# A two-block transformer kernel: one pass of squares for the norms between the blocks, and the context's tiles beside the second mixer's attention steps

## The reference

```python
def rmsnorm(x, g):
    return x * lax.rsqrt(jnp.mean(x * x, -1, keepdims=True) + EPS) * g

# first block, layer i = 1 (layer 0 has a gated short convolution in the place of the stick part)
p = rmsnorm(x, mix_norm[1]) @ b_in                     # 12 heads of stick queries, 4 of memory queries
kv = rmsnorm(x, kv_norm) @ w_kv_shared                 # stick keys and values
z = q @ k.T * scale                                    # stick-breaking attention, causal
log_not = where(causal, log_sigmoid(-z), 0)
tail = reversed_cumsum(log_not) - log_not
y_main = where(causal, exp(log_sigmoid(z) + tail), 0) @ v
y_mem = softmax(q_mem @ mem_k.T * scale) @ mem_v       # memory attention, 4 heads of 64
x = x + concat([y_main, y_mem]) @ w_o[1]
x = x + swiglu(rmsnorm(x, ffn_norm[1]), w_gate[1], w_up[1], w_down[1])
x = rmsnorm(x, final_norm)                             # end of the first block

# second block
sh1x, sc1x, ... = split(silu(c) @ w_ada + b_ada)       # six modulations of x,
sh1c, sc1c, ... = split(silu(c_ctx) @ w_ada + b_ada)   # two that matter of the context
hc = rmsnorm(ctx, norm1_g) * (1 + sc1c) + sh1c
s_f, s_b = context_states(hc)                          # lr, k and v projections of hc, a decayed sum
hx = rmsnorm(x, norm1_g) * (1 + sc1x) + sh1x
x = x + g1x * token_mixer(hx, s_f, s_b)                # begins with lr, k, q, v projections of hx
x = x + g2x * conv_ffn(rmsnorm(x, norm2_g) * (1 + sc2x) + sh2x)
return rmsnorm(x, final_norm_g)
```

## Time and profile before

| what | value |
|---|---|
| median of 3 runs (lowest, highest) | 1211.57 us (1210.45, 1211.79) |
| the profiled execution, its time | 1211.49 us |
| its span in the trace | 1210.2 us |
| PE busy | 1157.9 us, 96% |
| DVE busy | 833.1 us, 69% |
| ACT busy | 622.6 us, 51% |
| POOL busy | 149.4 us, 12% |
| granted TensorE clock, mean | 0.984 |
| DMA | 221.90 MB, mean 183 GB/s |

### The profile page before, as it was taken

One profiled execution on the slowest core, in us unless ns is written; L12 is line 12 of the kernel. 1 busy time (PEld: TensorE's weight loads), 2 busy tenths in 40 slices (PEclk: granted clock), 3 DMA queues, 4 the chain that ended last, 5 costly groups with the idle time before them and its releaser, 6 DMA issues.

```text
span 1210.2 us, 21837 instructions
## 1 busy us (share of the span) xinstructions
PE 1157.9 (96%) x9014; PEld 1110.4 (92%) x9014; DVE 833.1 (69%) x1278; ACT 622.6 (51%) x938; POOL 149.4 (12%) x111
## 2 busy tenths in 40 slices
PE   7999999999899899999999999999999989999996
PEld 6999999999788789999998898979899988999995
DVE  5677677778774756877787756577646767677775
ACT  5655444445564645444455664656437444555553
POOL 0003000000100012000000000000001032344431
PEclk9999999999999989999999999999999997999999
DMA  8655587776744144877877445354324552556550
GB/s 310 195 163 178 165 295 253 240 246 229 244 128 136 51 157 146 263 263 252 274 265 232 160 157 166 105 174 140 114 95 158 185 182 90 186 178 192 175 157 36
DMA packets 60467, 221.90 MB, mean 183 GB/s; under 512 B 6752, under 2 KB 7008, under 8 KB 59984
## 3 DMA queue, kind: packets, MB, share of 16 engines
q1 hardware_dynamic: 59904, 219.06, 55.0%
q10 hardware_dynamic: 288, 1.05, 0.2%
q0 software_dynamic: 176, 0.39, 0.1%
HBM read 219.42 MB, written 1.05 MB: 182 GB/s over the span
## 4 chain that ended last, share of the span: by engine, by line
PE 81%; DVE 10%; ACT 5%; issue 3%; DMA 1%; SPq 0%; POOL 0%; ACTq 0%; DVEq 0%
PE PS L350 23%; PE PS L352 22%; PE PS L351 22%; PE PS L355 13%; DVE w_lo L1316 4%; ACT w_hi L837 3%; DVE PS L1889 1%; DVE SQ L1587 1%; DMA ARENA<-memT 1%; DVE raw L1338 0%; DVE SQ L1352 0%; DVE ARENA L1352 0%; PE PS L455 0%; DVE H_lo L1362 0%; ACT ARENA L925 0%
## 5 line engine op out<-in xcount | busy, mean ns | idle before, releaser
L1316 DVE TENSOR_TENSOR w_lo<-raw,w_hi 128x1024 fp32r<-128x1024 f32 x325 | 398.8, 1228 | 259.9 <-ACT w_hi L837 259.4
L837 ACT ACTIVATE w_hi<-raw 128x1024 fp32r<-128x1024 f32 x356 | 372.5, 1054 | 141.7 <-PE PS L352 117.4
L350 PE MATMUL PS<-Y_hi,w_hi 128*128 128x256 f32 x1240 | 358.4, 289 | 9.6 <-DVE w_lo L1316 4.2
L351 PE MATMUL PS<-Y_lo,w_hi 128*128 128x256 f32 x1240 | 353.9, 285 | 0.0
L352 PE MATMUL PS<-Y_hi,w_lo 128*128 128x256 f32 x1240 | 353.8, 285 | 0.0
L350 PEld LDWEIGHTS PS<-Y_hi,w_hi 128*128 128x128 f32 x1240 | 240.8, 194 | 16.2 <-issue 9.4
L351 PEld LDWEIGHTS PS<-Y_lo,w_hi 128*128 128x128 f32 x1240 | 241.2, 194 | 0.4 <-issue 0.2
L352 PEld LDWEIGHTS PS<-Y_hi,w_lo 128*128 128x128 f32 x1240 | 241.0, 194 | 0.0
L350 PE MATMUL PS<-H_hi,w_hi 128*128 128x256 f32 x808 | 232.1, 287 | 5.3 <-DVE w_lo L1316 2.8
L351 PE MATMUL PS<-H_lo,w_hi 128*128 128x256 f32 x808 | 229.3, 284 | 0.0
L352 PE MATMUL PS<-H_hi,w_lo 128*128 128x256 f32 x808 | 229.2, 284 | 0.0
(11 more groups left out here) (206 smaller groups left out, 1316.7 us busy)
## 6 DMA issues: line engine op xcount, KB each, us to landing
raw<-stream SPq DMA_DIRECT2D x404, 512.0 KB, 4.2
ARENA<-memT SPq DMA_DIRECT2D x2, 512.0 KB, 7.7
X<-xT SPq DMA_DIRECT2D x1, 1024.0 KB, 11.4
ARENA<-c_rows SPq DMA_DIRECT2D x2, 512.0 KB, 8.2
ARENA<-memT SPq DMA_DIRECT2D x1, 1024.0 KB, 7.1
ARENA<-ctxT SPq DMA_DIRECT2D x1, 1024.0 KB, 8.1
outT<-ARENA SPq DMA_DIRECT2D x2, 512.0 KB, 2.6
CROW<-c_rows SPq DMA_DIRECT2D x1, 512.0 KB, 10.2
```

The lines of the kernel that those rows point to most:

```text
L350: pe.matmul(o, wh, xh, start=start, stop=False, skip_group_check=True)
L351: pe.matmul(o, wh, xl, start=False, stop=False, skip_group_check=True)
L837: act.activation(w_hi[n % RING][:], raw[at][:], ACT.Copy).then_inc(*mark("hi", n))
L1316: dve.tensor_tensor(w_lo[n % RING][:], raw[raw_of("slot", n)][:], w_hi[n % RING][:], ALU.subtract).then_inc(*mark("lo_dve", n))
```

## The change

**Tiles.** `ctx_lr` and `ctx_k` (5 slots) move from behind `ffn1` to behind `kv_v1`, where stick groups are still under way. `stick_output` becomes a paced generator `stick_outputs` (banks 2 and 3 instead of 4 to 6) that runs beside `stick_schedule`; `both(...)` steps two generators at once. `w_o1` takes its chunks in the order 0, 1, 2, 3, 6, 7, 4, 5.

**Memory attention** goes in halves: two maxima, two reciprocals, each transposed head waits for its own scalings, and the 8 exponentials are one step of ACT. `memory_attention(1)` starts at the first `b_q` tile, beside the norm of `kv`, and the stick groups now start at the first `kv_k` tile on every engine.

**Context.** The load of the context is issued among the slots of `a_c`; its sum of squares is beside `a_b`; its norm is behind the memory's in the tail of `ffn0`, which begins at j = 16 instead of 18, into memory of its own (`CX_hi`, `CX_lo`). All 16 modulations with two rows are the first 16 of `ffn0`; the second load and second silu of `CTX_ROW` in `ffn1` are gone.

**End of the first block.** `block1_end` takes one pass of squares. The weights of the sum, `PAIR`, are 1 in 16 columns and the square of the final norm's gain in 16 more, so that each quarter holds the sum of x^2 and of (gain x)^2; two matmuls with `HALVES` spread them. From both, ACT and DVE form the two inverse roots, and `norm1` is taken straight from X, with gain times final gain. The final norm of X itself (8 DVE operations) is `block1_output`, beside `context_states`. The norm stands beside 8 tiles (`ctx_v0`, `ctx_v1`) where 13 were.

```diff
-          ("kv_v1", 2), ("w_o1", KC), ("ffn1", FFN_SLOTS),
-          ("ctx_lr", 1), ("ctx_k", 4), ("ctx_v0", 4), ("ctx_v1", 4),
+          ("kv_v1", 2), ("ctx_lr", 1), ("ctx_k", 4), ("w_o1", KC), ("ffn1", FFN_SLOTS),
+          ("ctx_v0", 4), ("ctx_v1", 4),
...
+    if _l == 0:
+        _now = [_j] if _j < CTX_MODS else []
     else:
-        _now = [CTX_MODS + _one + i for i in range(2 if _l and _j in (11, 13, 15, 17) else 1)]
+        _now = [len(MOD_ORDER) + _i for _i in range(2 if _j % 2 and _j > 2 else 1)]
...
+def both(first, second):
+    live = [first, second]
+    while live:
+        live = [task for task in live if next(task, "end") != "end"]
+        if live:
+            yield
...
-                if (kind, n) == ("slot", AT["w_o1"] + RAW):
-                    sp.wait_ge(*past("am", NG - 1))
-                    sp.dma_start(CTX_ROW, c_rows[:, 1]).then_inc(*mark("c_in", 2, by=16))
-                if (kind, n) == ("slot", AT["b_qm"] + RAW - 1):
+                if (kind, n) == ("slot", AT["a_c"] + 4):
                     sp.dma_start(CTX, ctxT).then_inc(*mark("ctx_in", by=16))
...
             def memory_attention(l):        # PE
-                yield from nothing(6)
-                pe.wait_ge(*past("ma_prob", l, 7))
-                claim(*bs)
                 for h in range(MEMH):
+                    if h % 2 == 0:
+                        yield from pace.to(7 + l + h // 2)
+                    pe.wait_ge(*past("ma_prob", l, 2 * h + 1))
+                    claim(bs[h])
...
-            def stick_output():
+            def stick_outputs():
+                pace = Pace()
                 for c in range(MC):
-                    b = 4 + c // 2
+                    b = 2 + c // 2
                     if c % 2 == 0:
+                        yield from pace.to(14 + c)
                         claim(b)
...
             def block1_end():               # PE
-                yield
-                quarters("final")
-                yield
-                yield
-                sum_quarters("final")
-                yield
-                yield from nothing(5)
-                quarters("norm1")
-                yield
-                yield
-                sum_quarters("norm1")
-                yield from nothing(KC + 2)
+                pace = Pace()
+                yield from pace.to(4)
+                pe.wait_ge(*past("pair"))
+                claim(4, 5)
+                for k in range(KC):
+                    if k % 2 == 0:
+                        pe.wait_ge(*past("sq", "final", k // 2))
+                    row = 32 * (k % 4)
+                    last = mm(PS[row:row + 32, 4, 0:T], PAIR[:, k], SQ[:, k], k < 4, k >= 4)
+                last.then_inc(*mark("quarters", "final"))
+                yield from pace.to(6)
+                pe.wait_ge(*past("quartered", "final"))
+                for i in range(2):
+                    last = mm(PS[:, 4 + i, 0:T], HALVES[:, i], RS[:, 0])
...
-            ffn(0, Side(nothing(KC + 1)))
+            ffn(0)
...
             kept = 0
-            side.tasks[:0] = [nothing(1)]
-            side.tasks += [memory_attention(1), stick_schedule(stick_group, lambda: kept)]
+            side = Side(memory_attention(1), both(stick_schedule(stick_group, lambda: kept), stick_outputs()))
...
+            project("ctx_lr", 1, CX, lambda i: ("lr", 0), side, [norm_low("ctx", k) for k in range(KC)])
+            project("ctx_k", GH, CX, lambda i: ("kb", 0, i), side)
             side.finish()
-            pe.wait_ge(*past("vs", 1))
-            stick_output()
-            side = Side(context_rms())
...
             def block1_end():               # ACT
+                pace = Pace()
                 squares("final", X, [("x_add", 1, c) for c in range(KC // 2)])
+                yield from pace.to(4)
+                act.activation(RS[:, 0], PS[:, 4, 0:T], ACT.Copy).then_inc(*mark("quartered", "final"))
+                yield from pace.to(6)
+                act.activation(LR[:, 1], PS[:, 4, 0:T], ACT.Ln, bias=EPS_COL,
+                               scale=1.0 / (16 * D)).then_inc(*mark("rs_ln", "final"))
+                act.activation(RS[:, 1], LR[:, 1], ACT.Exp, scale=-1.0).then_inc(*mark("rs_square", "final"))
+                act.activation(RS[:, 0], LR[:, 1], ACT.Exp, scale=-0.5).then_inc(*mark("rs", "final"))
...
+                yield from pace.to(8)
                 yield from norm_his("norm1", H2, lambda c: SH1(c))
...
-            ffn(0, Side(memory_norm()))
+            ffn(0, Side(memory_norm(), context_norm()))
...
-            ffn(1, Side(context_norm()))
+            ffn(1, Side(pair_weights()))
 
             side = Side(block1_end())       # DVE
             side.step()
-            beside(13, side, 2)
+            beside(8, side, 2)
             side.finish()
-            side = Side(context_states())
+            side = Side(both(context_states(), block1_output()))
```

More of the change, by code:

```diff
@@ L52 @@
 for _l, _j in ((_l, _j) for _l in range(2) for _j in range(FC)):
[L53 to L56, removed]
+    if _l == 0:
+        _now = [_j] if _j < CTX_MODS else []
     else:
-        _now = [CTX_MODS + _one + i for i in range(2 if _l and _j in (11, 13, 15, 17) else 1)]
+        _now = [len(MOD_ORDER) + _i for _i in range(2 if _j % 2 and _j > 2 else 1)]
     MOD_ORDER += _now
     MODS_AFTER[AT[f"ffn{_l}"] + (RING + 1 + 2 * _j if _j < 2 else RING + 3 * _j)] = _now
-assert sorted(MOD_ORDER) == list(range(NMOD))
-CTX_FFN1 = next(a for a in MODS_AFTER[AT["ffn1"] + RING + 1])
+assert MOD_ORDER == list(range(NMOD))
 LOADS = []
@@ L223, in build @@
         LR = sb("LR", [P, 2, T])
-        ARENA = sb("ARENA", [P, 24832])
+        with ExitStack() as shared:
+            ARENA = shared.enter_context(nc.sbuf_tensor("ARENA", [P, 24832], F32))
+        sb("below", [P, 15488])
+        CX_lo, CX_hi = sb("CX_lo", [P, KC, T], F32R), sb("CX_hi", [P, KC, T], F32R)
+        CX = (CX_hi, CX_lo)
+        sb("above", [P, 24832 - 19584])
         def area(at, *shape):
@@ L278, in build @@
         RS_COLS = small[:, 32:34]
-        RS_AT = {"mem0": 1, "mix0": 0, "mix1": 0, "ctx": 1, "final": 0, "norm1": 1, "out": 0}
+        RS_OF = {"mem0": RS[:, 1], "mix0": RS[:, 0], "mix1": RS[:, 0], "ctx": LR[:, 1], "out": RS[:, 0]}
         def gain(name, c):
@@ L359, in slot, with tall @@
                 return n % RING
-            def tall(o, h, ready=None, within=None):
+            def tall(o, h, ready=None, within=None, order=range(KC)):
                 nonlocal n
                 r = slot()
-                for k in range(KC):
+                for k in order:
                     if ready:
@@ L387, in wide, with project @@
                 n += 1
-            def project(stage, count, h, release, side=None, ready=None, steps=1):
+            def project(stage, count, h, release, side=None, ready=None, steps=1, order=range(KC)):
                 assert n == AT[stage], (stage, n)
@@ L1223, in act_program @@
             act.dma_start(WS, sgu_wT).then_inc(*mark("late_in", 1, by=16))
-            side = Side(context_rms())
-            project("w_o1", KC, left, side, then=residual_square(1, H2, lambda c: gain("ffn1", c)))
-            side.finish()
+            project("w_o1", KC, left, then=residual_square(1, H2, lambda c: gain("ffn1", c)))
             inverse_rms("res1")
             act.preload_act_table(ACT.Silu)
-            ffn(1, Side(norm_his("ctx", Y2, lambda c: SH1(c, 1), CSQ)))
+            ffn(1)
             exp_set()
@@ L1560, in block1_end @@
                         yield
-                yield from nothing(3)
-                dve.wait_ge(*past("x_final", KC - 1))
-                yield from norms("norm1", X, lambda c: GS[:, 1, c:c + 1], ("norm1", RS[:, 1]), H2,
-                                 lambda c: SH1(c))
             def log_decays(s, tmp, pace, steps):
```

248 lines of the change are left out of this document (134 added, 114 removed).

## The result

The changed kernel takes 1213.29 us (median of 20 runs, 1211.85 to 1215.04) where the kernel before takes 1211.14 (20 runs, 1207.44 to 1214.21). The ratio is 1.0020, with a 95% interval of 1.0013 to 1.0027: about 2 us slower, where 9 us faster was forecast and the range ended at 1209. The profiled execution of the changed kernel took 1214.23 us and its span is 1212.9, 2.7 more than before.

The account below looks back on a forecast made before the run. PE was taken as the bound, busy 1157.9 of 1210.2 us, so only its waits and slow-clock stretches could be won. Terms -4.5 - 2.8 - 0.1 - 1.9 - 1.4 + 1.0 + 0.8 = -8.9 took 1211.5 to 1202.6 us; range 1194 to 1209.

Parts of the forecast that it names:

- Memory attention in halves: At the memory attention's transposes and outputs: halves let transposes start after two heads, cutting a 5.4 us loss; -2.8, bounds -4.5 and -1.
- Tiles beside the stick groups: Between kv_k and w_o1: five context tiles fill PE's untiled stretch, 10.3 of 14.8 us loss staying; -4.5, bounds -14 and +0.
- Rival 1: At the stick groups: tiles cover them fully and tails do not wait, 8 us less, 1194.6 us; chance 0.18.
- End of the first block: At block1_end: one pass of squares saves 3.4 us, a new wait for Y_lo costs 3.3; -0.1, bounds -2.0 and +2.6.
- Rival 2: At the first block's end: norms starved, last Y_lo late by 6 instead of 3.3, 1208.9 us; chance 0.15.
- The context's sum of squares: Moved from w_o1 to a_b: claimed the same PE work, so nothing.
- The FFNs: Fewer modulations and silus: ffn1's start -1.9 us, ffn0's end -1.4, and ffn0's start +1.0 for a double modulation.
- The final norm beside the states: X's final norm, 8 DVE operations, beside context_states: only the fourth pair costs; +0.8 us, bounds 0 and 3.
- Rival 3: From kv_k to w_o1: waits of 1.4 us at every group hold the clock at 0.82; +15, 1217.6 us; chance 0.07.

## Why the prediction was wrong

**Memory attention in halves (-2.8): right.** A loss of 5.5 is now 2.8 (1.69 at the transposes with their start, 0.92 and 0.15 behind): -2.7. I had 1.9 at the transposes and 0.7 at the outputs; the traces have waits of 1.54 and 0.67.

**Tiles beside the stick groups (-4.5): a term mis-sized.** It is -0.2 (the -2.9 of the stretch less the -2.7 above), inside the bounds of -14 and 0. The mechanism was right and is what the tables of the order had shown: each of the tails 1 to 4 waits 1.38, 1.26, 1.26, 1.17 for L1522, forecast as 1.4. What I had too small, in the main, stands around it: z of group 1 lost 1.1 (forecast 0.5, for a copy out; its releaser is ACT's ln of group 0, and in two other traces DVE's mask), the last tails waited 2.47 and then ran at a low clock, 3.38 in the place of 1.67 (4.3, forecast 2.3), and each of eight more changes from a group's matmuls to a tile costs some 0.15 (a tile of 3.04 behind tails, 385.32 to 388.36, against 2.88), which I had not counted. The 1.7 of low clock behind the last tails is not in every execution: the trace of norm1 at step 9 is 1.5 better there, so that the term would have come out at -1.7. I had also read the stretch before wrongly: it holds three z (409.29, 414.46 and 420.17) and not two. The work at full clock is 13.6 and the loss 13.9, and with 10.3 to stay the term would have been -3.6; some 13.7 stayed. Rival 1 was as wrong as my forecast, but what it would give is real: with DVE one step earlier the stretch is 12 us shorter.

**End of the first block (-0.1): the step that failed.** The wait of 3.3 for `Y_lo` is there, 3.0, and the saving of 3.4 is there, as the run with the tiles put back shows. I priced the wait as time idle alone. Behind it came 4.8 us more: the `lr` tile took 7.12 for 2.97 (3.0 of it waits), the decay products 3.71 for 1.92, the next tile 4.90 for 3.06. Some 4.2 of it is slow matmuls, and goes with the wait when norm1 starts at step 7; the rest is the start behind each wait. The earlier trace rows had shown this (0.81 behind a wait of 3.77, which I charged with 1.4 us there), and I left it out here. Forecast -0.1 with an upper bound of +2.6, measured +4.7. Rival 2 had the place and at 1208.9 too small a price, by the same omission.

**The context's sum of squares (nothing): wrong, a term put at nothing without a price.** "The same PE work" came to +3.1 in `a_b`, and `w_o1` gave back 0.6. In `w_o1` the pass had cost 2.0, but its leaving was nearly undone by two waits that took its place, for H_lo (0.59) at its start and X (0.81) behind it:

```profile
452.09 0.38 PE L359 MATMUL PS<-H_hi,w_hi 128*128 128x256 f32 x1 [0.59 <-DVE H_lo L1541]
...
475.47 0.38 PE L359 MATMUL PS<-Y_hi,w_hi 128*128 128x256 f32 x1 [0.81 <-DVE X L1440]
```

**The FFNs (-1.9, -1.4, +1.0): right.** -1.8, -1.6 and +0.7; PE's wait of 1.30 at the start of `ffn1` is 0.35, that at `ffn0`'s end is gone.

```profile
488.01 0.36 PE L359 MATMUL PS<-Y_hi,w_hi 128*128 128x256 f32 x1 [0.35 <-DVE w_lo L1330]
```

**The final norm beside the states (+0.8): +0.4**, a wait of 0.37 ahead of the one of 1.18.

**Rival 3 (clock):** its place was wrong. From 366 to 430 the clock is 1.00, with waits of 1.2 to 1.4 at the tails of groups 1 to 4; it falls behind the single waits of 2.2 to 2.5, here that of the last tails.

```profile
366.00:430.00 64.00, 57.13 (x404) 50.75 (x404) 37.31 (x53) 36.11 (x48) 0.00 (x0) 1.00 0.35 116
430.00:440.00 10.00, 7.53 (x51) 6.53 (x49) 5.39 (x9) 2.06 (x3) 0.00 (x0) 0.83 0.31 107
```

In numbers: forecast -8.9, measured +2.7 between the traces. The 11.6 between are 4.8 at the block's end, 4.3 at the groups, 2.5 for the squares, 1.4 of clock at 797 whose cause is open, less 1.4 of small lines.

## What to carry to other kernels

When code is moved in a schedule of in-order queues, compare on each engine which tile every step stands behind, before and after: one step of one engine was worth over 10 us here, more than the 8.9 that the whole change was to bring. Price a wait of 2 to 3 us on TensorE with the slow matmuls that may stand behind it: here they cost 4.2 us behind waits of 3.0, and 1.5 or nothing behind a wait of 2.5. And take a deadline earlier by the fill that a step stands behind, not by the number of the step.

## What the runs showed of the hardware

A wait of 2.24 us behind two short ones left TensorE's matmuls 0.21 us apart, in the place of 0.12, for 8.7 us (granted clock 0.74 from 690 to 710), while four waits of 1.2 to 1.4 us, 10 us apart, left it at 1.00 (366 to 430).

The same wait is not always followed by the same clock. In two traces whose kernels are the same up to there, a wait of 2.47 us was followed by tails of 3.38 us in one (clock 0.83 from 430 to 440) and of 1.92 in the other (1.00), and a wait of 2.2 us by a clock of 0.83 in one and 1.00 in the other (130 to 140).
